# Unread transposes of the identity on the matmul engine while row norms are formed

## The chip, the cores and the metric

The kernel runs on one core of a Trainium2 chip. The metric is the device time of one execution in microseconds. TensorE (PE) multiplies matrices, VectorE (DVE) and ScalarE (ACT) do the elementwise work, GpSimd (POOL) here only forms powers, and SyncE (SP) issues the weight loads. [...]

## The reference

Two blocks of two layers each run over x of 256 rows by 1024 columns, all in float32. The joints of this case lie in the second block:

```
def second_block(x, ...):
    for l in range(DEPTH):                       # DEPTH = 2
        h = rms_norm_2(x, mix_pre_norm[l])
        m = hybrid_mixer(h, w_in[l], ...)        # 256x1024 -> 256x1024
        x = x + rms_norm_2(m, mix_post_norm[l])
        h = rms_norm_2(x, ffn_pre_norm[l])
        x = x + rms_norm_2(swiglu(h, ffn_gate[l], ffn_up[l], ffn_down[l]), ffn_post_norm[l])
    return x

def rms_norm_2(x, w):
    return x * rsqrt(mean(x * x, axis=-1) + 1e-6) * w
```

The mixer projects h to 13 groups of columns and more, runs a gated delta rule, a retention and a pooling branch, and multiplies their gated sum by w_out. Between the last product of one part and the first of the next lies a chain on which nothing else depends: row norm of the result, addition to x, row norm of x, transposition, scaling by the gain.

## The kernel before, in words

Each engine has its own program, and semaphores tie them together; nothing reorders an engine's list. x lies in SBUF as two tiles of 128 rows (t = 0 and 1). Weights come in units of four 128x512 pieces through a ring of slots that SP fills. Where precision asks for it, ACT rounds a unit (the `_hi` part, L954) and DVE subtracts it from the original (the `_rest` part, L1286), and PE then forms three products instead of one in `split_part` (L531 for groups whose result lies by column, L540 for the others). Each pair of the unit's pieces is a part, counted by the semaphore `w_split`.

PSUM has four banks `gp` for the large products and four banks `mp` for small steps. Small steps have names; `ORDER_1` and `ORDER_2` list them in the order in which PE runs them. The step with number n uses bank n % 4, and `begin` lets PE wait until the step n - 4 has been read (`step_read`). `end` raises `step_done` for the reader.

`x_transposes` carries out a joint on PE: the steps xT0, xT1 (tile t = 0, four 128x128 transposes each) when DVE has normed that tile (`x_normed`), xT2, xT3 for tile t = 1, and at its end it waits until all four banks are read. The steps fT0 to fT3 are the same before the feed-forward part. After it PE waits for `h_split`, then runs the matmuls of the next group (Q or F0, L531).

The other engines at a joint: DVE adds the result to x (`add_result`), ACT squares the rows (L961 and L1152), POOL forms the inverse root (L1916), and DVE scales the tile (L1402), reads each transposed step from PSUM with the gain (`normed_T`, L1280), and splits it into a rounded part and a rest (L1327, L1286), which raises `h_split`. In layer 0's first joint DVE reads xT0 and xT1 only after it has normed both tiles; at the other three it reads the first pair inside `add_result`, ahead of the norm of tile 1.

The last product before a joint runs t = 0 first and t = 1 second (`tail`, `split_tail`), so that tile 0 of x is ready while PE still works on tile 1.

Of the kernel before, what the change touches and what calls it, by code (L numbers as in the profile page):

```python
# [6 lines left out]
P = 128  # L7
# [4 lines left out]
DEPTH = 2  # L12
# [78 lines left out]
for _n, _name in enumerate(("do_g", "mq_g", "mk_g", "ho_g")):  # L91
# [6 lines left out]
    + ["om0", "om1", "hgo0", "hgo1"] + [f"sc{h}" for h in range(4)] + ["yT4", "yT5"] + [f"sc{h}" for h in range(4, 8)] + ["yT2", "yT3"] \  # L98
    + [f"pt{h}" for h in range(8)] + ["oa0", "oa1", "yT0", "yT1"]
BETWEEN = {1: ["rqT0", "rqT1", "rkT0", "rkT1"], 2: ["rs0", "rs1", "rs2"], 3: ["ro0", "ro1"], 4: ["pm0", "pm1"], 5: ["py0", "py1"]}  # L100
ORDER_2 = [f"xT{i}" for i in range(4)] + ["ba", "cg", "gb0", "gb1"] \
    + [f"bT{j}{t}" for j in range(3) for t in range(2)] \
    + ["kT0", "kT1", "qT0", "qT1", "kbT0", "kbT1", "mm0", "mm1", "at0", "at1"] \
    + ["mi0", "mi1"] \
# [1 line left out]
       for step in [f"{s}{n}_{t}" for s in ("Y", "Z", "W") for t in range(2) if not (s == "Z" and n == len(LEVELS) - 1)]  # L106
       + BETWEEN.get(n, [])] \
    + ["oT_r0", "oT_r1", "u0", "wT", "st", "vn1", "do0", "do1", "oT_d0", "oT_d1"] \
    + [f"yT{i}" for i in range(4)] + [f"fT{i}" for i in range(4)]
PRE = ["colA", "memT0", "memT1", "memT2", "memT3", "colB"]  # L110
STEPS = PRE + [f"A{l}.{s}" for l in range(DEPTH) for s in ORDER_1] + [f"B{l}.{s}" for l in range(DEPTH) for s in ORDER_2]
STEP_NO = {s: n for n, s in enumerate(STEPS)}
# [73 lines left out]
def mixer_program(nc, w, out):  # L186
# [6 lines left out]
    with ctx:  # L193
# [34 lines left out]
        ident, upper, ones = C("ident"), C("upper"), C("ones")  # L228
# [54 lines left out]
        xT3, cT3, e3 = region(b_x, 12, S), region(b_c, 12, S), region(b_e, 12, S)  # L283
# [11 lines left out]
        xs2 = region(b_e, TT, D)  # L295
# [42 lines left out]
        step_read = [sem(f"step_read{i}") for i in range(4)]  # L338
# [18 lines left out]
        def bank(step, *dims):  # L357
            v = mp[:, STEP_NO[step] % 4]
            if len(dims) == 2:
                n = dims[0] * dims[1]  # L360
                return v[:, 0:n].rearrange("p (a b) -> p a b", a=dims[0])
            return v[:, 0:dims[0]] if dims else v
# [114 lines left out]
        def _(pe):  # L477
            state = {"unit": 0, "step": 0}

            def begin(step, *waits):  # L480
                n = STEP_NO[step]
                assert n == state["step"], (step, STEPS[state["step"]])
                state["step"] += 1
                if n >= 4:
                    pe.wait_ge(step_read[n % 4], n // 4)
                for wait in waits:
                    pe.wait_ge(*wait)

            def end(ins):
                ins.then_inc(step_done, 1)  # L490
# [96 lines left out]
                    if t == 0:  # L587
                        last.then_inc(sig("first_tile"), 1)

            def x_transposes(names, src, n):  # L590
                for i in range(4):
                    t, q = divmod(i, 2)
                    transposes(names(i), [src[:, t, (4 * q + j) * P:(4 * q + j + 1) * P] for j in range(4)],
                               (sig("x_normed"), 2 * n + t + 1))
                for i in range(4):
                    pe.wait_ge(*read_out(names(i)))
# [13 lines left out]
            for l in range(DEPTH):  # L610
                s = lambda n: f"A{l}.{n}"
# [124 lines left out]
            for l in range(DEPTH):  # L736
                s = lambda n: f"B{l}.{n}"

                def group_in(g):
                    n = GROUP_NO[s(g)]  # L740
                    return group_read[n % 2], n // 2 + 1
                x_transposes(lambda i: s(f"xT{i}"), xs2, DEPTH + 2 * l)
                pe.wait_ge(sig("h_split"), 2 * TT * l + TT)
                for g in "QKV":
                    split_units(s(g), 2)
# [2 lines left out]
                for t in range(TT):  # L748
                    for k in range(KD):
                        for i, h_part in enumerate((mix_hT_hi, mix_hT_rest)):  # L750
                            last = nc.tensor.matmul(bank(s("ba"))[:, 16 * t:16 * t + 16], h_part[:, t, k, :], w_ba_parts[:, l, k, :],
                                                    start=(k == 0 and i == 0), stop=(k == KD - 1 and i == 1))
# [7 lines left out]
                for t in range(TT):  # L760
                    begin(s(f"gb{t}"), (sig("gates_ready"), l + 1))
                    for h in range(NH):
                        last = nc.tensor.matmul(bank(s(f"gb{t}"))[:, P * h:P * h + P], gbc[:, NH * t + h, :], upper, start=True, stop=True)
# [106 lines left out]
                last = len(LEVELS) - 1  # L870
# [35 lines left out]
                        pe.wait_ge(*read_out(s(f"yT{2 * j + t}")))  # L906
                sum_transposes(0)
                tail(4, lambda k, t: reg("B", f"G{2 + k // 4}")[:, t, P * (k % 4):P * (k % 4) + P], {2: lambda: sum_transposes(1)})
                x_transposes(lambda i: s(f"fT{i}"), xs2, DEPTH + 2 * l + 1)
                pe.wait_ge(sig("h_split"), 2 * TT * (l + 1))  # L910
                for j in range(FF_G):
                    split_units(s(f"F{j}"), 2)
# [1026 lines left out]
```

## Time and profile before

| | |
|---|---|
| median of 3 runs | 1636.79 us (1632.76 to 1643.85) |
| profiled execution, its own time | 1637.35 us |
| span of the profiled execution | 1635.5 us |
| PE busy | 1479.7 us, 90% |
| DVE busy | 966.3 us, 59% |
| ACT busy | 675.1 us, 41% |
| mean granted clock of PE | 0.958 |

PE's busy time includes matmuls that overlap, so their spacing in the timeline tells the pace and not the duration of one. An idle time in brackets stands before the instruction that ended it, with what released it.

The four joints are called A (before layer 0 of the second block, near 535 us), B (before layer 0's feed-forward part, near 880 us), C (before layer 1, near 1085 us) and D (before layer 1's feed-forward part, near 1430 us).

### The profile page before, as it was taken

Reading aid. Unit: us, or ns where it says so; the run is one execution under the profiler, and the core shown is the slowest. Engines: PE = TensorE matmul, PEld = TensorE weight load, DVE = VectorE, ACT = ScalarE, POOL = GpSimd, SP = SyncE. Lnnn points to the kernel's source line nnn. Section 1 sums busy time; section 2 is a strip of 40 time slices with the busy share of each in tenths; the row PEclk is TensorE's granted clock in tenths of the full one; section 3 lists DMA queues with packets and bytes.
Section 4 is the critical chain, followed back from the end, with each engine's and each line's share of the span. In section 5 each row is a group of like instructions: output and inputs, shape, how many; then the busy total and the mean of one; then the engine's idle time right before and its main releaser. Section 6 shows DMA issues by size and latency. Waiting matters only on the chain.

```text
span 1635.5 us, 20210 instructions
## 1 busy us (share of the span) xinstructions
PE 1479.7 (90%) x8410; PEld 1249.1 (76%) x8410; DVE 966.3 (59%) x1133; ACT 675.1 (41%) x901; POOL 50.2 (3%) x41
## 2 busy tenths in 40 slices
PE   5999987979889797999997999969889999889997
PEld 4977776868768786788654999869668866389986
DVE  7588664579664566755525566453885534265644
ACT  4565554465563455432213333325644221233332
POOL 0002000000100000000000000000000000000000
PEclk9999998989999898999998999989999999989999
DMA  7444223434333543333343655535333334435653
GB/s 247 156 130 152 78 83 123 157 127 134 100 102 116 174 154 104 103 104 108 124 154 111 186 186 188 181 119 171 129 103 104 122 109 163 146 109 186 186 176 115
DMA packets 138986, 225.80 MB, mean 138 GB/s; under 512 B 7889, under 2 KB 54289, under 8 KB 138769
## 3 DMA queue, kind: packets, MB, share of 16 engines
q1 hardware_dynamic: 133456, 221.60, 41.3%
q10 hardware_dynamic: 5440, 2.93, 0.6%
q8 instruction: 67, 1.10, 0.3%
q14 instruction: 23, 0.18, 0.0%
HBM read 223.46 MB, written 1.05 MB: 137 GB/s over the span
## 4 chain that ended last, share of the span: by engine, by line
PE 76%; DVE 13%; ACT 6%; issue 4%; POOL 1%; ACTq 0%; DMA 0%; POOLq 0%; DVEq 0%
PE gp L540 33%; PE gp L531 23%; PE gp L513 5%; PE mp L784 5%; PE gp L583 3%; DVE wt_rest L1286 3%; PE mp L630 2%; PE mp L495 2%; DVE arena L1722 2%; DVE arena L1280 2%; DVE hT L1280 1%; ACT arena L1028 1%; ACT arena L1168 1%; POOL rs_out L1916 1%; PE mp L684 1%
## 5 line engine op out<-in xcount | busy, mean ns | idle before, releaser
L531 PE MATMUL gp<-hT_hi,wt_hi 128*128 128x256 f32 x704 | 200.8, 285 | 6.9 <-DVE hT_rest L1286 6.9
L531 PE MATMUL gp<-hT_rest,wt_hi 128*128 128x256 f32 x704 | 200.4, 285 | 0.0
L531 PE MATMUL gp<-hT_hi,wt_rest 128*128 128x256 f32 x704 | 200.3, 284 | 0.0
L1286 DVE TENSOR_TENSOR wt_rest<-wt,mix_hi 128x1024 fp32r<-128x1024 f32 x120 | 141.5, 1221 | 96.5 <-ACT mix_hi L954 95.8
L1286 DVE TENSOR_TENSOR wt_rest<-wt,wt_hi 128x1024 fp32r<-128x1024 f32 x132 | 155.5, 1221 | 69.1 <-ACT wt_hi L954 69.1
L954 ACT ACTIVATE wt_hi<-wt 128x1024 fp32r<-128x1024 f32 x132 | 132.1, 1051 | 117.5 <-DMA wt<-in_ffn_up 58.8
L1286 DVE TENSOR_TENSOR wt_rest<-wt,first_hi 128x1024 fp32r<-128x1024 f32 x120 | 142.8, 1221 | 59.1 <-ACT first_hi L954 58.3
L954 ACT ACTIVATE first_hi<-wt 128x1024 fp32r<-128x1024 f32 x120 | 123.9, 1059 | 111.7 <-PE gp L540 98.1
L540 PE MATMUL gp<-mix_hi,mix_hT_hi 128*128 128x512 f32 x384 | 157.0, 409 | 4.3 <-DVE wt_rest L1286 4.3
L540 PE MATMUL gp<-wt_rest,mix_hT_hi 128*128 128x512 f32 x384 | 155.4, 405 | 0.0
L954 ACT ACTIVATE mix_hi<-wt 128x1024 fp32r<-128x1024 f32 x120 | 122.3, 1059 | 77.8 <-PE gp L540 48.0
L540 PE MATMUL gp<-mix_hi,mix_hT_rest 128*128 128x512 f32 x384 | 151.9, 396 | 0.0
L531 PEld LDWEIGHTS gp<-hT_hi,wt_hi 128*128 128x128 f32 x704 | 136.4, 194 | 7.7 <-issue 7.7
L495 PE MATMUL mp<-const,arena 128*128 128x128 f32 x512 | 81.4, 313 | 66.1 <-DVE arena L1402 25.4
L531 PEld LDWEIGHTS gp<-hT_rest,wt_hi 128*128 128x128 f32 x704 | 136.5, 194 | 0.0
L531 PEld LDWEIGHTS gp<-hT_hi,wt_rest 128*128 128x128 f32 x704 | 136.4, 194 | 0.0
L495 PEld LDWEIGHTS mp<-const,arena 128*128 128x128 f32 x512 | 69.2, 162 | 81.0 <-issue 45.9
L1280 DVE TENSOR_TENSOR arena<-arena,gp 128x512 f32<-128x512 f32 (+1 forms) x56 | 44.9, 802 | 136.3 <-ACT arena L1260 80.0
L934 ACT ACTIVATE arena<-gp 128x1024 f32<-128x1024 f32 x48 | 49.1, 1023 | 166.0 <-PE gp L540 166.0
L540 PE MATMUL gp<-first_hi,first_hT_hi 128*128 128x512 f32 x256 | 105.4, 412 | 4.2 <-DVE wt_rest L1286 4.2
L540 PE MATMUL gp<-wt_rest,first_hT_hi 128*128 128x512 f32 x256 | 103.6, 405 | 0.0
L540 PE MATMUL gp<-first_hi,first_hT_rest 128*128 128x512 f32 x256 | 102.5, 400 | 0.0
(270 smaller groups left out, 2890.5 us busy)
## 6 DMA issues: line engine op xcount, KB each, us to landing
wt<-in_w_in SPq DMA_DIRECT2D x100, 1024.0 KB, 5.1
wt<-in_ffn_gate SPq DMA_DIRECT2D x44, 512.0 KB, 3.9
wt<-in_ffn_up SPq DMA_DIRECT2D x44, 512.0 KB, 4.9
wt<-in_w_out SPq DMA_DIRECT2D x20, 1024.0 KB, 5.1
wt<-in_ffn_down SPq DMA_DIRECT2D x20, 1024.0 KB, 5.0
wt<-in_w_mem_kv SPq DMA_DIRECT2D x8, 1024.0 KB, 5.1
wt<-in_w_branch_pool SPq DMA_DIRECT2D x4, 1024.0 KB, 5.0
wt<-in_w_branch_ret SPq DMA_DIRECT2D x4, 1024.0 KB, 5.0
```

Source lines behind the costliest of these rows:

```text
L495: last = nc.tensor.transpose(bank(step)[:, P * j:P * j + P], tile, ident)
L513: last = nc.tensor.matmul(group_bank(group, t), stationary(k0 + k, t), wt[:, u % SLOTS, k, :], start=(k0 + k == 0), stop=(k0 + k == GROUPS ...
L531: last = nc.tensor.matmul(o, a[:, k, P * c:P * c + P], b[:, :, k0 + k, :], start=(k0 + k == 0 and c % 2 == 0 and i == 0), stop=(k0 + k == ...
L540: last = nc.tensor.matmul(group_bank(group, t), a, b[:, k, :], start=(kk == k_first and i == 0), stop=(kk == k_last and i == 2))
L583: last = nc.tensor.matmul(group_bank(GROUPS[g][0], t), stationary(k0 + k, t), wt[:, u % SLOTS, k, :], start=(k0 + k == 0), stop=(k0 + k == ...
L630: last = nc.tensor.matmul(bank(s(f"hg{n}_{t}"))[:, P * h:P * h + P], src_k[:, h, kt * P:kt * P + P], src_q[:, h, t * P:t * P + P], start=T ...
L784: last = nc.tensor.matmul(bank(step)[:, P * h:P * h + P], lhs(h), rhs(h), start=True, stop=True)
L934: nc.scalar.activation(dst, group_banks(name), func).then_inc(group_read[GROUP_NO[name] % 2], 1)
L954: nc.scalar.activation(rounded_part(u)[:, k:k + nk, :], wt[:, u % SLOTS, k:k + nk, :], ACT.Copy)\
L1280: return nc.vector.tensor_tensor(o, i0, i1, ALU.mult)
L1286: return nc.vector.tensor_tensor(o, i0, i1, ALU.subtract)
L1722: ins = nc.vector.scalar_tensor_tensor(cT3[:, k, d:], xT3[:, k, 0:S - d], taps[:, 3 - d, k:k + 1], cT3[:, k, d:], ALU.mult, ALU.add)
```

## The change

A new helper `keep_busy` transposes the identity into a bank of its own a given number of times. It is called between the second and third transposing step of each joint in the second block, and again behind the fourth. Two steps are added to the order at each joint, which shifts the bank numbers of the steps behind them. Nothing reads what `keep_busy` writes; its last pass itself raises `step_read`.

```
--- before.py
+++ after.py
@@ -98,7 +98,7 @@
     + ["om0", "om1", "hgo0", "hgo1"] + [f"sc{h}" for h in range(4)] + ["yT4", "yT5"] + [f"sc{h}" for h in range(4, 8)] + ["yT2", "yT3"] \
     + [f"pt{h}" for h in range(8)] + ["oa0", "oa1", "yT0", "yT1"]
 BETWEEN = {1: ["rqT0", "rqT1", "rkT0", "rkT1"], 2: ["rs0", "rs1", "rs2"], 3: ["ro0", "ro1"], 4: ["pm0", "pm1"], 5: ["py0", "py1"]}
-ORDER_2 = [f"xT{i}" for i in range(4)] + ["ba", "cg", "gb0", "gb1"] \
+ORDER_2 = ["xT0", "xT1", "xw0", "xT2", "xT3", "xw1"] + ["ba", "cg", "gb0", "gb1"] \
     + [f"bT{j}{t}" for j in range(3) for t in range(2)] \
     + ["kT0", "kT1", "qT0", "qT1", "kbT0", "kbT1", "mm0", "mm1", "at0", "at1"] \
     + ["mi0", "mi1"] \
@@ -106,7 +106,7 @@
        for step in [f"{s}{n}_{t}" for s in ("Y", "Z", "W") for t in range(2) if not (s == "Z" and n == len(LEVELS) - 1)]
        + BETWEEN.get(n, [])] \
     + ["oT_r0", "oT_r1", "u0", "wT", "st", "vn1", "do0", "do1", "oT_d0", "oT_d1"] \
-    + [f"yT{i}" for i in range(4)] + [f"fT{i}" for i in range(4)]
+    + [f"yT{i}" for i in range(4)] + ["fT0", "fT1", "fw0", "fT2", "fT3", "fw1"]
 PRE = ["colA", "memT0", "memT1", "memT2", "memT3", "colB"]
 STEPS = PRE + [f"A{l}.{s}" for l in range(DEPTH) for s in ORDER_1] + [f"B{l}.{s}" for l in range(DEPTH) for s in ORDER_2]
 STEP_NO = {s: n for n, s in enumerate(STEPS)}
@@ -587,8 +587,19 @@
                     if t == 0:
                         last.then_inc(sig("first_tile"), 1)
 
-            def x_transposes(names, src, n):
+            def keep_busy(step, passes):
+
+                begin(step)
+                for j in range(passes):
+                    last = nc.tensor.transpose(bank(step)[:, P * (j % 4):P * (j % 4) + P], ident, ident)
+                    if j == passes - 2:
+                        end(last)
+                last.then_inc(step_read[STEP_NO[step] % 4], 1)
+
+            def x_transposes(names, src, n, between=None):
                 for i in range(4):
+                    if i == 2 and between is not None:
+                        between()
                     t, q = divmod(i, 2)
                     transposes(names(i), [src[:, t, (4 * q + j) * P:(4 * q + j + 1) * P] for j in range(4)],
                                (sig("x_normed"), 2 * n + t + 1))
@@ -739,7 +750,8 @@
                 def group_in(g):
                     n = GROUP_NO[s(g)]
                     return group_read[n % 2], n // 2 + 1
-                x_transposes(lambda i: s(f"xT{i}"), xs2, DEPTH + 2 * l)
+                x_transposes(lambda i: s(f"xT{i}"), xs2, DEPTH + 2 * l, lambda: keep_busy(s("xw0"), 40 if l else 14))
+                keep_busy(s("xw1"), 28)
                 pe.wait_ge(sig("h_split"), 2 * TT * l + TT)
                 for g in "QKV":
                     split_units(s(g), 2)
@@ -906,7 +918,8 @@
                         pe.wait_ge(*read_out(s(f"yT{2 * j + t}")))
                 sum_transposes(0)
                 tail(4, lambda k, t: reg("B", f"G{2 + k // 4}")[:, t, P * (k % 4):P * (k % 4) + P], {2: lambda: sum_transposes(1)})
-                x_transposes(lambda i: s(f"fT{i}"), xs2, DEPTH + 2 * l + 1)
+                x_transposes(lambda i: s(f"fT{i}"), xs2, DEPTH + 2 * l + 1, lambda: keep_busy(s("fw0"), 40))
+                keep_busy(s("fw1"), 16)
                 pe.wait_ge(sig("h_split"), 2 * TT * (l + 1))
                 for j in range(FF_G):
                     split_units(s(f"F{j}"), 2)

```

PE's list at joint C before, from the first transposing step to the next group (`step_read` with a digit is the semaphore of that bank):

```order
L495 MATMUL mp<-const,arena 128x128 [waits x_normed,step_read3]
L495 MATMUL mp<-const,arena 128x128 x3
L495 MATMUL mp<-const,arena 128x128 [waits x_normed,step_read0]
L495 MATMUL mp<-const,arena 128x128 x3
L495 MATMUL mp<-const,arena 128x128 [waits x_normed,step_read1]
L495 MATMUL mp<-const,arena 128x128 x3
L495 MATMUL mp<-const,arena 128x128 [waits x_normed,step_read2]
L495 MATMUL mp<-const,arena 128x128 x3
L531 MATMUL gp<-mix_hT_hi,mix_hi_54 128x256 [waits h_split,step_read2,group_read0,step_read1,w_split,step_read0,step_read3]
```

And with the change:

```order
L495 MATMUL mp<-const,arena 128x128 [waits x_normed,step_read3]
L495 MATMUL mp<-const,arena 128x128 x3
L495 MATMUL mp<-const,arena 128x128 [waits x_normed,step_read0]
L495 MATMUL mp<-const,arena 128x128 x3
L594 MATMUL mp<-const 128x128 [waits step_read1]
L594 MATMUL mp<-const 128x128 x39
L495 MATMUL mp<-const,arena 128x128 [waits x_normed,step_read2]
L495 MATMUL mp<-const,arena 128x128 x3
L495 MATMUL mp<-const,arena 128x128 [waits x_normed,step_read3]
L495 MATMUL mp<-const,arena 128x128 x3
L594 MATMUL mp<-const 128x128 [waits step_read3,step_read2,step_read0]
L594 MATMUL mp<-const 128x128 x27
L531 MATMUL gp<-mix_hT_hi,mix_hi_54 128x256 [waits w_split,group_read0,h_split]
```

Forty passes stand before the second pair and 28 behind it; the waits for the reads of the first three or four banks (`step_read3`, `step_read2`, `step_read0`), which stood before the group's first matmul, now stand before the 28 passes, and the fourth transposing step waits for `step_read3`, the bank of the first.

At joint A, with the change:

```order
L495 MATMUL mp<-const,arena 128x128 [waits x_normed,step_read0]
L495 MATMUL mp<-const,arena 128x128 x3
L495 MATMUL mp<-const,arena 128x128 [waits x_normed,step_read1]
L495 MATMUL mp<-const,arena 128x128 x3
L594 MATMUL mp<-const 128x128 [waits step_read2]
L594 MATMUL mp<-const 128x128 x13
L495 MATMUL mp<-const,arena 128x128 [waits x_normed,step_read3]
L495 MATMUL mp<-const,arena 128x128 x3
L495 MATMUL mp<-const,arena 128x128 [waits x_normed,step_read0]
L495 MATMUL mp<-const,arena 128x128 x3
L594 MATMUL mp<-const 128x128 [waits step_read0,step_read3,step_read1]
L594 MATMUL mp<-const 128x128 x27
L531 MATMUL gp<-mix_hT_hi,mix_hi_54 128x256 [waits w_split,group_read0,h_split]
```

Here the first filler has 14 passes. The fourth transposing step waits for `step_read0`, the bank of this joint's first step.

## Rows read from the trace of the kernel before

**Rows 1.** The page: busy time, and the chain that ended last by engine.

```profile
PE 1479.7 (90%) x8410; PEld 1249.1 (76%) x8410; DVE 966.3 (59%) x1133; ACT 675.1 (41%) x901; POOL 50.2 (3%) x41
...
PE 76%; DVE 13%; ACT 6%; issue 4%; POOL 1%; ACTq 0%; DMA 0%; POOLq 0%; DVEq 0%
```

**Rows 2.** Timeline, PE at A to D: start us, us, engine, line, operation, count [idle before <-releaser].

```profile
535.62 1.94 PE L495 MATMUL mp<-const,arena 128*128 128x128 f32 x8 [3.38 <-DVE arena L1402]
...
543.38 0.55 PE L531 MATMUL gp<-mix_hT_hi,mix_hi 128*128 128x256 f32 x1 [5.82 <-DVE wt_rest L1286]
...
875.90 1.04 PE L495 MATMUL mp<-const,arena 128*128 128x128 f32 x8
...
884.26 1.94 PE L495 MATMUL mp<-const,arena 128*128 128x128 f32 x8 [7.33 <-DVE arena L1402]
...
889.68 0.55 PE L531 MATMUL gp<-hT_hi,wt_hi 128*128 128x256 f32 x1 [3.48 <-DVE hT_rest L1286]
...
1086.09 1.94 PE L495 MATMUL mp<-const,arena 128*128 128x128 f32 x8 [7.39 <-DVE arena L1402]
...
1093.75 0.55 PE L531 MATMUL gp<-mix_hT_hi,mix_hi 128*128 128x256 f32 x1 [5.72 <-DVE mix_hT_rest L1286]
...
1433.78 1.94 PE L495 MATMUL mp<-const,arena 128*128 128x128 f32 x8 [7.33 <-DVE arena L1402]
...
1439.17 0.55 PE L531 MATMUL gp<-hT_hi,wt_hi 128*128 128x256 f32 x1 [3.45 <-DVE hT_rest L1286]
```

**Rows 3.** Windows around joints A to D: stretch, busy us of each engine, PEclk, DMA.

```profile
535.00:547.00 12.00, 5.56 (x25) 5.22 (x26) 11.43 (x13) 2.65 (x3) 0.00 (x0) 0.50 0.36 132
...
880.00:892.00 12.00, 4.26 (x19) 3.92 (x20) 11.14 (x14) 6.83 (x8) 0.54 (x1) 0.50 0.06 20
...
893.00:895.00 2.00, 2.00 (x19) 2.00 (x18) 2.00 (x3) 0.00 (x0) 0.00 (x0) 1.00 0.03 8
...
1084.00:1097.00 13.00, 5.19 (x23) 4.85 (x24) 10.83 (x13) 2.10 (x4) 0.54 (x1) 0.50 0.07 21
...
1429.00:1442.00 13.00, 4.77 (x21) 4.43 (x22) 12.10 (x15) 6.83 (x8) 0.54 (x1) 0.50 0.10 34
```

**Rows 4.** Timeline, PE, matmuls of L531 in joint A.

```profile
543.73 0.41 PE L531 MATMUL gp<-mix_hT_rest,mix_hi 128*128 128x256 f32 x1
...
547.57 0.41 PE L531 MATMUL gp<-mix_hT_rest,mix_hi 128*128 128x256 f32 x1
...
548.33 0.28 PE L531 MATMUL gp<-mix_hT_hi,mix_hi 128*128 128x256 f32 x1
...
551.25 0.28 PE L531 MATMUL gp<-mix_hT_rest,mix_hi 128*128 128x256 f32 x1
```

**Rows 5.** Timeline, VectorE (DVE): last reads of transposed tiles in A, B, C.

```profile
538.70 1.41 DVE L1280 TENSOR_TENSOR hT<-mp,cols 128x512 f32<-128x512 f32 x2
...
885.89 1.41 DVE L1280 TENSOR_TENSOR hT<-mp,cols 128x512 f32<-128x512 f32 x2
...
1089.99 1.41 DVE L1280 TENSOR_TENSOR hT<-mp,cols 128x512 f32<-128x512 f32 x2
```

**Rows 6.** One line, L495: count, duration of one in ns, minimum/median/maximum.

```profile
L495 PE MATMUL mp<-const,arena x512: 270/273/477, 6.9 to 1435.3; 128*128 128x128 f32 x171
```

**Rows 7.** Timeline, PE, transposes elsewhere in the mixer of layer 0.

```profile
628.13 2.82 PE L495 MATMUL mp<-const,arena 128*128 128x128 f32 x12 [2.47 <-ACT arena L1200]
...
647.50 4.18 PE L495 MATMUL mp<-const,arena 128*128 128x128 f32 x24 [4.24 <-DVE arena L1280]
...
658.25 1.07 PE L495 MATMUL mp<-const,arena 128*128 128x128 f32 x8 [2.37 <-DVE arena L1280]
```

**Rows 8.** Windows over the stretches of rows 7.

```profile
628.00:633.00 5.00, 4.87 (x18) 4.39 (x19) 0.00 (x0) 4.63 (x8) 0.00 (x0) 0.50 0.00 0
...
647.00:650.00 3.00, 2.50 (x12) 2.53 (x13) 3.00 (x4) 1.12 (x2) 0.00 (x0) 0.50 0.23 89
...
651.00:652.00 1.00, 0.68 (x7) 0.45 (x5) 0.48 (x1) 1.00 (x3) 0.00 (x0) 1.00 0.06 16
```

More of the change, by code:

```diff
@@ L100 @@
 BETWEEN = {1: ["rqT0", "rqT1", "rkT0", "rkT1"], 2: ["rs0", "rs1", "rs2"], 3: ["ro0", "ro1"], 4: ["pm0", "pm1"], 5: ["py0", "py1"]}
-ORDER_2 = [f"xT{i}" for i in range(4)] + ["ba", "cg", "gb0", "gb1"] \
+ORDER_2 = ["xT0", "xT1", "xw0", "xT2", "xT3", "xw1"] + ["ba", "cg", "gb0", "gb1"] \
     + [f"bT{j}{t}" for j in range(3) for t in range(2)] \
@@ L108 @@
     + ["oT_r0", "oT_r1", "u0", "wT", "st", "vn1", "do0", "do1", "oT_d0", "oT_d1"] \
-    + [f"yT{i}" for i in range(4)] + [f"fT{i}" for i in range(4)]
+    + [f"yT{i}" for i in range(4)] + ["fT0", "fT1", "fw0", "fT2", "fT3", "fw1"]
 PRE = ["colA", "memT0", "memT1", "memT2", "memT3", "colB"]
@@ L588, in tail, with keep_busy, x_transposes @@
                         last.then_inc(sig("first_tile"), 1)
-            def x_transposes(names, src, n):
+            def keep_busy(step, passes):
+                begin(step)
+                for j in range(passes):
+                    last = nc.tensor.transpose(bank(step)[:, P * (j % 4):P * (j % 4) + P], ident, ident)
+                    if j == passes - 2:
+                        end(last)
+                last.then_inc(step_read[STEP_NO[step] % 4], 1)
+            def x_transposes(names, src, n, between=None):
                 for i in range(4):
+                    if i == 2 and between is not None:
+                        between()
                     t, q = divmod(i, 2)
@@ L741, in group_in @@
                     return group_read[n % 2], n // 2 + 1
-                x_transposes(lambda i: s(f"xT{i}"), xs2, DEPTH + 2 * l)
+                x_transposes(lambda i: s(f"xT{i}"), xs2, DEPTH + 2 * l, lambda: keep_busy(s("xw0"), 40 if l else 14))
+                keep_busy(s("xw1"), 28)
                 pe.wait_ge(sig("h_split"), 2 * TT * l + TT)
@@ L908, in _ @@
                 tail(4, lambda k, t: reg("B", f"G{2 + k // 4}")[:, t, P * (k % 4):P * (k % 4) + P], {2: lambda: sum_transposes(1)})
-                x_transposes(lambda i: s(f"fT{i}"), xs2, DEPTH + 2 * l + 1)
+                x_transposes(lambda i: s(f"fT{i}"), xs2, DEPTH + 2 * l + 1, lambda: keep_busy(s("fw0"), 40))
+                keep_busy(s("fw1"), 16)
                 pe.wait_ge(sig("h_split"), 2 * TT * (l + 1))
```

## The prediction

> **What bounds the kernel now.** I read the page first: the matmul engine (PE) is busy for 90% of the span, and the chain that ended last runs on PE for 76% of it [rows 1]. So PE's own pace and its idle time at the joints set the end. Then I read PE in order of time around the four joints that the change touches. I call them A (into layer 0 of the second block), B (into layer 0's feed-forward part), C (into layer 1) and D (layer 1's feed-forward part). Each has the same shape: eight transposes right behind the last matmul, idle, eight transposes, idle, then the dense matmuls of L531 [rows 2]. The first idle stretch is 3.38 us in A and 7.33 to 7.39 us in the others. The second is 5.82, 3.48, 5.72 and 3.45 us.
>
> [...] What half a clock costs shows in the spacing of the L531 matmuls: 18 steps from 543.73 to 547.57 us are 0.213 us each, 25 steps from 548.33 to 551.25 us are 0.117 us each [rows 4]. So each matmul issued at half clock loses 0.096 us. In A the half-clock matmuls last from 543.38 to about 547.9 us, which is 21 of them; in C, where the stretch at 0.50 reaches past 1097 us, from 1093.75 to about 1097.4 us, 17; in B from 889.68 to about 892.7 us, 14; in D I take 14 too, since it starts like B. That is 66 such matmuls, **6.4 us, the most that a held clock could give back**. The slow second group of transposes (1.94 us for eight against 1.04 us [rows 2]) costs nothing: VectorE reads it only later, at 538.70, 885.89 and 1089.99 us [rows 5].
>
> **What is added.** 222 transposes: 14 + 28 in A, 40 + 16 in B, 40 + 28 in C, 40 + 16 in D. Eight existing ones take 1.04 us and one alone 0.27 us, so the seven steps between them are 0.110 us each at the full clock; at half clock eight take 1.94 us and one 0.48 us, 0.209 us a step, and I take the 0.213 us of the matmuls [rows 2, 4, 6]. Nothing reads the results, so a pass costs only what it delays on PE.
>
> *First filler (14 or 40 passes).* At full clock, where it starts because PE was dense until then, it takes 1.5 us in A (room 3.38) and 4.4 us in B, C and D (room 7.3). It delays nothing. At half clock throughout, 40 passes would be 8.5 us, 1.2 us more than the room, and half of that would reach VectorE, which takes the tile 1.6 us after its release in B [rows 2, 5]; behind dense work I take the full clock and cost it at nothing. The extra step also moves the PSUM bank of the steps behind it: the last of the four real transposes now waits until the first one's bank is read. VectorE reads that bank while the second pair is being prepared, or sooner, so this is nothing as well.
>
> *Second filler (28 or 16 passes).* It stands behind the waits for all four reads, so it can't start when PE goes idle, only when VectorE has read the last bank: 538.70 + 1.41 = 540.1 us in A, 887.3 us in B, 1091.4 us in C [rows 5]. From there to the first matmul of before there are 3.2, 2.4 and 2.35 us; D is as B. At 0.110 us, 28 passes are 3.1 us and 16 are 1.8 us: covered in A, B and D, but **0.75 us too long in C**. At half clock 28 passes are 6.0 us and 16 are 3.4 us, and all four joints are late, by 2.7, 1.0, 3.6 and 1.0 us. Behind the filler on PE stand the matmuls, and behind these the whole chain; no other engine waits for the filler.
>
> **Does the clock stay up?** With the filler at full clock PE's idle times become: A 1.9, then 3.5 us before the second filler; B and D 2.9, then 2.0; C 3.0, then 4.3. The trace has comparable gaps. 2.37 us of idle behind dense work left the clock up: the eight transposes after it take 1.07 us. 2.47 us elsewhere did not, nor did 3.38 and 4.24 us [rows 2, 7, 8]. So in A and C I expect the clock to fall in the second gap, which the change leaves open, and in B and D it is a toss-up. Once down, transposes alone do bring it back: 24 of them start at 647.50 us at 0.50, and it is at 1.00 by 651 us [rows 7, 8]. From the start of work to the return it is about 3 us there, about 3, 4 and 4.5 us in B, C and A, and over 5 us at 628 us; I take 3.7 us.
>
> [...]
>
> **The sum, joint by joint.**
> - A, clock down: 17 passes in 3.7 us, 11 more at 0.110 us, so the filler ends at 545.05. The 21 matmuls then run at full clock to 547.5; before, they ended at 543.38 + 21 x 0.213 = 547.85. **-0.35 us**.
> - C, clock down: the filler ends at 1096.3, 17 matmuls end at 1098.3 against 1097.4 before. **+0.9 us**.
> - B: with the clock held, 14 x 0.096 = -1.35 us. With it down, 16 half-clock passes end at 890.7, one half-clock matmul and 13 at full clock end at 892.45 against 892.65: -0.2 us. Half and half: **-0.8 us**. D the same, **-0.8 us**.
>
> Together -1.05 us. Nothing downstream takes it back or adds to it, as PE runs on without a wait after each joint for tens of microseconds. Made against the profiled execution, 1637.35 us becomes 1636.3 us; that execution stands 0.56 us above the median of 1636.79 us, so the median would be 1635.7, **about 1636 us: no change that can be measured**. A measurement of this kernel tells about 1% from no change, 16 us, and all cases lie inside it.
>
> **The rivals.**
> 1. *The clock is held at all four joints.* For it: 2.37 us of idle was bridged, and both fillers shorten the gaps. Against: 3.5 and 4.3 us stay open in A and C. It gives -2.0 in A, -1.35 in B and in D, and -1.65 + 0.75 = -0.9 in C: -5.6 us, **1631 us**.
> 2. *Slower: transposes of the identity neither hold nor restore the clock, so the second filler runs at half clock and is itself the delay.* The matmuls behind it start slow as before. It decides as soon as a pass takes over 0.115 us in A, 0.147 us in B and D (cover by number of passes); C is past its point already. Price 2.7 + 1.0 + 3.6 + 1.0 = +8.3 us, **1645 us**. [...] Against it: the 24 transposes at 647.50 us; for it, only that those read data and these read one constant tile.
> 3. *The passes are slow at any clock*, because weights and moving data come from the same 128 columns of SBUF, which no row shows. The same +8.3 us, but dense filler holds or restores the clock, -6.4 us: about +2 us, **1639 us**.
>
> **Numbers.** Chances: the sum 0.60, rival 1 0.20, rival 2 0.12, rival 3 0.08. The runs differ among themselves: half-clock stretches elsewhere in the kernel fall anew in each execution, and the three runs of before span 1632.76 to 1643.85 us; so each case has some 3 us on either side. The range of 1629 to 1643 us takes in the first, most of the second and the last, and leaves out the larger part of rival 2. Faster by over 1% (below 1620 us) would take more than twice what the slow matmuls cost in all: 0.02. Slower by over 1% (above 1653 us) takes rival 2 and more: 0.03. Within 1%: 0.95.
>
> **What would show it.** 222 transposes that read only the constants; the first filler of 14 or 40 at 0.110 us a pass; the second starting right behind VectorE's last read of a transposed tile; in A and C a clock of 0.50 when it starts and of 1.00 when L531 starts, with L531 1.7 and 2.6 us later behind that read than before; in B and D either a clock of 1.00 throughout or a fall in the second gap. Spacing of the first L531 matmuls at 0.117 us shows that the clock came back. I am wrong if the spacing of the filler is not 0.110 us at full clock, if a new wait of VectorE on PE appears at the bank that is used again, or if the gain or loss lies outside these four joints.

## The result, and the profile after

| | before | changed |
|---|---|---|
| median of 20 runs each | 1637.47 us | 1643.67 us |
| lowest to highest | 1632.76 to 1643.85 | 1639.22 to 1649.91 |
| ratio, 95% interval | | 1.0036, 1.0023 to 1.0049 |
| span of the profiled execution | 1635.5 us | 1644.4 us |

The change costs about 6 us (3.8 to 8.0 us by the interval). That is less than the 1% named in the prediction, but its sign is clear of the noise, and the median lies 0.7 us above the range that was given. Two executions far above all the others, one of the kernel before at 1830.8 us and one of a variant below at 5264 us, are in no ratio.

The page of the changed kernel, its busy line, answers to [rows 1]: 222 more matmuls and as many more weight loads, 30 us more of busy time for each, and no other engine moved by more than 1 us.

```profile
PE 1509.3 (92%) x8632; PEld 1278.6 (78%) x8632; DVE 966.4 (59%) x1133; ACT 675.5 (41%) x901; POOL 49.2 (3%) x41
```

The timeline of PE in joints A, B and C of the changed kernel answers to [rows 2] (the columns are the same; D is as B; L594 is the filler):

```profile
533.50 1.69 PE L594 MATMUL mp<-const 128*128 128x128 f32 x14
537.05 1.16 PE L495 MATMUL mp<-const,arena 128*128 128x128 f32 x8 [1.86 <-DVE arena L1415]
541.79 5.29 PE L594 MATMUL mp<-const 128*128 128x128 f32 x28 [3.58 <-DVE hT L1293]
...
881.27 4.53 PE L594 MATMUL mp<-const 128*128 128x128 f32 x40
888.77 1.06 PE L495 MATMUL mp<-const,arena 128*128 128x128 f32 x8 [2.96 <-DVE arena L1415]
892.07 3.65 PE L594 MATMUL mp<-const 128*128 128x128 f32 x16 [2.24 <-DVE hT L1293]
...
1083.86 4.53 PE L594 MATMUL mp<-const 128*128 128x128 f32 x40
1091.62 1.48 PE L495 MATMUL mp<-const,arena 128*128 128x128 f32 x8 [3.22 <-DVE arena L1415]
1097.18 5.77 PE L594 MATMUL mp<-const 128*128 128x128 f32 x28 [4.09 <-DVE hT L1293]
```

The first fillers run at full clock: 40 passes take 4.53 us, 0.11 us each. The second pair of transposes in B then runs at full clock too (1.06 us, not 1.94). But PE idles again until VectorE's last read, and the second filler takes 3.65 us for 16 passes, 0.213 us each. The windows over these stretches, with the same columns as [rows 3], say why (PEclk, the last figure but two, is the granted clock as a share of full speed): in B the clock is at 1.00 beside the first filler and the transposes and at 0.50 beside the second filler, and it is at 0.50 beside the second filler of A and C too.

```profile
541.00:546.00 5.00, 4.21 (x20) 4.24 (x21) 4.93 (x6) 0.00 (x0) 0.00 (x0) 0.50 0.00 0
547.00:549.00 2.00, 2.00 (x19) 2.00 (x18) 1.06 (x1) 0.00 (x0) 0.00 (x0) 1.00 0.00 0
881.00:886.00 5.00, 4.80 (x44) 4.56 (x42) 3.35 (x6) 1.13 (x5) 0.54 (x1) 1.00 0.79 261
889.00:890.00 1.00, 0.83 (x8) 0.59 (x6) 0.96 (x2) 1.00 (x2) 0.00 (x0) 1.00 0.00 0
891.00:897.00 6.00, 4.93 (x23) 4.96 (x24) 5.90 (x7) 1.56 (x2) 0.00 (x0) 0.50 0.00 1
898.00:900.00 2.00, 2.00 (x19) 2.00 (x18) 2.00 (x3) 0.00 (x0) 0.00 (x0) 1.00 0.00 0
1092.00:1102.00 10.00, 5.91 (x30) 5.54 (x29) 9.05 (x10) 0.00 (x0) 0.00 (x0) 0.51 0.00 0
```

So in B the filler pushes the first L531 matmul to 895.37 us, 15.0 us behind the joint's first transpose (13.8 before), and the matmuls still begin at half clock, ten of them:

```profile
895.37 0.56 PE L531 MATMUL gp<-hT_hi,wt_hi 128*128 128x256 f32 x1
895.73 0.41 PE L531 MATMUL gp<-hT_rest,wt_hi 128*128 128x256 f32 x1
...
897.85 0.28 PE L531 MATMUL gp<-hT_hi,wt_hi 128*128 128x256 f32 x1
897.97 0.28 PE L531 MATMUL gp<-hT_rest,wt_hi 128*128 128x256 f32 x1
```

To follow the 6 us I cut the span into parts, from starts on PE's timeline. A *joint* is the time from its first transpose to the 60th matmul behind its first L531 matmul; behind the joints lie *mixer 0* (A to B), *mixer 1* (C to D) and the two feed-forward stretches. These, from B to C and from D to the start of PE's last matmul, were 179.39 and 179.16 us within 0.01 us in every profile and are left out. The table has all eight profiles of the two kernels and those of the variants below, in us.

| profile | A | B | C | D | joints | mixer 0 | mixer 1 |
|---|---|---|---|---|---|---|---|
| before | 21.34 | 22.37 | 24.87 | 22.37 | 90.95 | 323.36 | 322.88 |
| before, 2nd | 21.08 | 23.56 | 25.57 | 22.44 | 92.65 | 326.84 | 323.57 |
| before, 3rd | 20.99 | 22.37 | 24.88 | 22.39 | 90.63 | 322.88 | 322.84 |
| before, 4th | 21.35 | 22.37 | 25.13 | 23.54 | 92.39 | 323.37 | 326.78 |
| changed | 21.48 | 23.20 | 26.82 | 23.15 | 94.65 | 326.29 | 323.65 |
| changed, 2nd | 21.45 | 23.16 | 26.96 | 23.09 | 94.66 | 326.36 | 323.59 |
| changed, 3rd | 21.45 | 23.16 | 26.96 | 23.08 | 94.65 | 326.32 | 323.64 |
| changed, 4th | 21.47 | 23.24 | 26.90 | 23.32 | 94.93 | 326.26 | 326.62 |
| steps only | 21.09 | 23.40 | 25.50 | 22.34 | 92.33 | 326.88 | 323.68 |
| first filler only | 21.02 | 22.21 | 24.88 | 22.25 | 90.36 | 322.92 | 322.98 |
| second filler only | 21.30 | 23.04 | 26.83 | 23.08 | 94.25 | 323.39 | 323.62 |
| second filler short | 19.82 | 22.39 | 24.94 | 22.36 | 89.51 | 324.75 | 322.90 |
| second filler early | 19.28 | 22.52 | 24.85 | 22.34 | 88.99 | 323.96 | 323.45 |
| second filler doubled | 24.13 | 24.94 | 28.97 | 24.99 | 103.03 | 326.46 | 326.36 |
| dense | 19.28 | 21.03 | 23.39 | 21.05 | 84.75 | 326.17 | 325.71 |
| dense, 2nd | 19.28 | 21.03 | 23.57 | 21.06 | 84.94 | 323.96 | 322.81 |
| dense, mixers too | 19.46 | 21.03 | 23.18 | 21.04 | 84.71 | 323.02 | 322.39 |

By the means of four profiles each, the change adds 0.27, 0.52, 1.80 and 0.47 us in A to D, 3.1 us together, and 2.2 and 0.4 us in the two mixers. The stretch ahead of joint A, which the change doesn't touch, was 530.4 us before and 531.5 after, with 529.4 to 532.6 among the eight; four profiles a side can't tell this 1.1 us from chance.

### The profile page after: what moved, and what is told of

It reads as the page before. It is cut to its first block, busy times and chain, and to the rows that moved or that the text cites. A ratio compares the mean times of both kernels' runs of the same rounds, so it can differ in the third digit from the quotient of the medians.

```text
span 1644.4 us, 20654 instructions
## 1 busy us (share of the span) xinstructions
PE 1509.3 (92%) x8632; PEld 1278.6 (78%) x8632; DVE 966.4 (59%) x1133; ACT 675.5 (41%) x901; POOL 49.2 (3%) x41
## 3 DMA queue, kind: packets, MB, share of 16 engines
HBM read 223.46 MB, written 1.05 MB: 137 GB/s over the span
## 4 chain that ended last, share of the span: by engine, by line
PE 77%; DVE 12%; ACT 5%; issue 3%; POOL 1%; ACTq 0%; DMA 0%; POOLq 0%; DVEq 0%
PE gp L540 33%; PE gp L531 22%; PE gp L513 5%; PE mp L796 4%; PE gp L583 3%; DVE wt_rest L1299 3%; PE mp L495 2%; PE mp L641 2%; DVE arena L1735 2%; DVE arena L1293 2%; PE mp L594 1%; DVE hT L1293 1%; ACT arena L1041 1%; POOL rs_out L1929 1%; PE mp L695 1%
## 5 line engine op out<-in xcount | busy, mean ns | idle before, releaser
L531 PE MATMUL gp<-hT_hi,wt_hi 128*128 128x256 f32 x704 | 200.4, 285 | 0.0
L531 PE MATMUL gp<-hT_rest,wt_hi 128*128 128x256 f32 x704 | 200.0, 284 | 0.0
L531 PE MATMUL gp<-hT_hi,wt_rest 128*128 128x256 f32 x704 | 200.0, 284 | 0.0
L540 PE MATMUL gp<-mix_hi,mix_hT_hi 128*128 128x512 f32 x384 | 157.7, 411 | 4.4 <-DVE wt_rest L1299 4.4
L540 PE MATMUL gp<-wt_rest,mix_hT_hi 128*128 128x512 f32 x384 | 155.9, 406 | 0.0
L540 PE MATMUL gp<-mix_hi,mix_hT_rest 128*128 128x512 f32 x384 | 152.2, 396 | 0.0
L531 PEld LDWEIGHTS gp<-hT_hi,wt_hi 128*128 128x128 f32 x704 | 136.2, 194 | 0.0
L531 PEld LDWEIGHTS gp<-hT_rest,wt_hi 128*128 128x128 f32 x704 | 136.0, 193 | 0.0
L531 PEld LDWEIGHTS gp<-hT_hi,wt_rest 128*128 128x128 f32 x704 | 136.0, 193 | 0.0
L495 PE MATMUL mp<-const,arena 128*128 128x128 f32 x512 | 79.7, 309 | 51.4 <-DVE arena L1293 13.2
L495 PEld LDWEIGHTS mp<-const,arena 128*128 128x128 f32 x512 | 67.9, 159 | 66.3 <-issue 31.4
L540 PE MATMUL gp<-first_hi,first_hT_hi 128*128 128x512 f32 x256 | 105.5, 412 | 4.2 <-DVE wt_rest L1299 4.2
L540 PE MATMUL gp<-wt_rest,first_hT_hi 128*128 128x512 f32 x256 | 103.5, 404 | 0.0
L540 PE MATMUL gp<-first_hi,first_hT_rest 128*128 128x512 f32 x256 | 102.5, 400 | 0.0
```

The source lines that it names most:

```text
L495: last = nc.tensor.transpose(bank(step)[:, P * j:P * j + P], tile, ident)
L531: last = nc.tensor.matmul(o, a[:, k, P * c:P * c + P], b[:, :, k0 + k, :], start=(k0 + k == 0 and c % 2 == 0 and i == 0), stop=(k0 + k == ...
L540: last = nc.tensor.matmul(group_bank(group, t), a, b[:, k, :], start=(kk == k_first and i == 0), stop=(kk == k_last and i == 2))
```

## The experiments

Theory 1: the second filler, which can start only when VectorE has read the last bank, meets a clock that has just fallen, runs at half clock for longer than the time that hides it, and delays all behind it. The rivals were the added steps and waits themselves, and work on PE that slows the chain beside it. All edits are against the changed kernel, and each ratio is against the kernel before as it ran beside the variant: 12 executions of each variant (5 of the doubled one, 7 of the last one), 12 to 35 of the kernel before.

**Steps only.** Fillers of 2 passes.

```
-  lambda: keep_busy(s("xw0"), 40 if l else 14)); keep_busy(s("xw1"), 28)
+  lambda: keep_busy(s("xw0"), 2));               keep_busy(s("xw1"), 2)
   ... fw0, fw1 likewise 2
```

> Both fillers of every joint cut to 2 passes (16 instead of 222 in all), so that the two added steps, the moved bank numbers and the moved waits stay, and the work goes. Theory 1 (the second filler, which starts only behind VectorE's last read and then runs at half clock, is what is late): within 2 us of the kernel before, each joint from its first transpose to the 60th L531 matmul within 0.3 us of before (21.3, 22.4, 24.9, 22.4 us). Rival 2 (the steps and waits themselves cost, through the banks of the mixer): +5 to +6 us as with the change. Rival 3 (PE work in the first gap slows the chain beside it): as before, since there is none.

Measured: ratio 1.0007 (0.9993 to 1.0022). The added steps, their waits and the moved banks cost nothing that can be seen. The joints of this one profile came out 1.4 us above the first profile of before and not within 0.3 us each; the second and fourth profiles of the kernel before show the same 92.4 to 92.7 us.

**First filler only.**

```
-  keep_busy(s("xw1"), 28)   keep_busy(s("fw1"), 16)
+  keep_busy(s("xw1"), 2)    keep_busy(s("fw1"), 2)
```

> The first filler of each joint as in the change (14 or 40 passes), the second cut to 2. Theory 1: within 2 us of before; the clock still falls in the second gap of each joint, and the first L531 matmuls run at half clock as before. Rival 2: +5 to +6 us. Rival 3 (the first filler slows ScalarE, VectorE or the weight loads beside it): +3 us or more, with a longer stretch from the first to the third transposing step than 11.5 us less 3.1 us in B.

Measured: 1.0000 (0.9986 to 1.0014), joints 90.36 us. The first filler is free, and useless: the clock falls behind it, in the second gap (in B 10.0 us behind the joint's first transpose, with the gap from 9.4 to 11.7 us). Its 134 passes beside the norms delay nothing: in B the second pair of transposes starts 8.4 us behind the first, as before.

**Second filler only.**

```
-  keep_busy(s("xw0"), 40 if l else 14)   keep_busy(s("fw0"), 40)
+  keep_busy(s("xw0"), 2)                 keep_busy(s("fw0"), 2)
```

> The second filler as in the change (28 or 16 passes), the first cut to 2. Theory 1: nearly all of the change's cost, +4 to +6 us; the joints from first transpose to the 60th L531 matmul 0.1, 0.8, 1.9 and 0.8 us longer than before in A to D, because the passes run at 0.213 us. Rival 2: +5 to +6 us too, but then the first variant shows it as well. Rival 3: within 2 us of before.

Measured: 1.0029 (1.0014 to 1.0043), 4.7 us, with joints of 94.25 us. The cost of the change in the joints is here, and joint by joint it is that of the change within 0.2 us. In this variant the clock falls in the first gap already. In B it has been down for 5.1 us when the filler starts at 887.01 us, and it is at half for 5.1 us more:

```profile
887.01 3.65 PE L594 MATMUL mp<-const 128*128 128x128 f32 x16 [1.36 <-DVE hT L1293]
```

```profile
882.00:892.00 10.00, 6.93 (x32) 6.59 (x33) 9.20 (x11) 5.50 (x6) 0.54 (x1) 0.50 0.01 2
893.00:895.00 2.00, 2.00 (x19) 2.00 (x18) 2.00 (x3) 0.00 (x0) 0.00 (x0) 1.00 0.00 0
```

**Second filler doubled.**

```
-  keep_busy(s("xw1"), 28)   keep_busy(s("fw1"), 16)
+  keep_busy(s("xw1"), 56)   keep_busy(s("fw1"), 32)
```

> The change with its second filler doubled (56 and 32 passes). Theory 1: the passes stand in PE's list with nothing beside them, so all that is added is paid: 28 more passes at the full clock, to which it has come back by then, are +3.1 us in A and in C, and 16 more are about +1.9 us in B and D; +10 us on the change, +16 us on the kernel before, ratio about 1.010. Were the cost in the added steps or in the first filler, doubling the second would change nothing: ratio 1.003 to 1.004.

Measured: 1.0089 (1.0070 to 1.0108), 14.6 us. The joints are 8.4 us above those of the change. In B and D the 16 added passes are paid in full at 0.11 us, +1.8 us each. In A and C the 28 added passes cost 2.7 and 2.1 us and not 3.1, because in this profile the clock returned earlier, at 12.5 and 17.4 us behind the joint's first transpose instead of 13.3 and 19.3.

**Second filler short.**

```
-  keep_busy(s("xw1"), 28)                  keep_busy(s("fw1"), 16)
+  keep_busy(s("xw1"), 10 if l else 14)     keep_busy(s("fw1"), 10)
```

> The first filler as in the change, the second cut to what fits behind VectorE's last read at half clock: 14 passes (3.0 us) in A and 10 (2.1 us) in B, C and D. Theory 1: L531 starts as early as before in every joint, and the clock returns 1 to 2 us earlier for it, so 1 to 4 us faster than before (1633 to 1636 us). Rival 2: +4 to +6 us. Rival 3: +3 us.

Measured: 0.9992 (0.9979 to 1.0006); joints 89.51 us. No delay is left. The gain I had expected with it, an earlier return of the clock, appears in A alone (19.82 us); in B, C and D the joints are as before.

**Second filler early**, with the same numbers of passes, ahead of the waits for the reads.

```
 def x_transposes(names, src, n, between=None, behind=None):
     ...
+    if behind is not None:
+        behind()                  # the second filler
     for i in range(4):
         pe.wait_ge(*read_out(names(i)))
```

> The change with its own numbers of passes (14 and 28, 40 and 16, 40 and 28, 40 and 16), only the second filler moved ahead of the four waits for VectorE's reads. Theory 1: the second filler then runs at full clock right behind the transposes and ends 2.6 to 3.6 us before the matmuls are released, so it delays nothing; the clock still falls behind it in most joints or shortly before L531. No cost, and none or little gain: ratio 0.998 to 1.0005. If instead the number of passes itself were what costs, wherever they stand: +3 to +6 us as with the change.

Measured: 0.9991 (0.9979 to 1.0002). The very 222 passes of the change cost nothing once the second filler stands ahead of the waits: in B its 16 passes take 1.91 us, and 2.58 us of idle are left ahead of the release of L531. A gains (19.28 us); in B, C and D the clock falls within 1 us of the start of L531 (0.3 and 0.8 us behind it in B and C, 0.4 us ahead of it in D), and the joints are as before.

```profile
881.68 1.07 PE L495 MATMUL mp<-const,arena 128*128 128x128 f32 x8 [2.96 <-DVE arena L1417]
882.58 1.91 PE L594 MATMUL mp<-const 128*128 128x128 f32 x16
887.08 0.36 PE L531 MATMUL gp<-hT_hi,wt_hi 128*128 128x256 f32 x1 [2.58 <-DVE hT_rest L1301]
```

**Dense.** The same place, with as many passes as the gaps hold at full clock.

```
-  lambda: keep_busy(s("xw0"), 40 if l else 14)), keep_busy(s("xw1"), 28)
+  lambda: keep_busy(s("xw0"), 60 if l else 26), lambda: keep_busy(s("xw1"), 54))
-  lambda: keep_busy(s("fw0"), 40)),              keep_busy(s("fw1"), 16)
+  lambda: keep_busy(s("fw0"), 60),              lambda: keep_busy(s("fw1"), 36))
```

> The second filler is moved ahead of the four waits for VectorE's reads, so that it starts right behind the fourth transposing step, and both fillers are sized to fill their gaps at full clock: 26 and 54 passes in A, 60 and 36 in B, 60 and 54 in C, 60 and 36 in D. Theory 1 (gaps of 2 us and more let the clock fall, and only that makes a pass dear): the clock stays at 1.00 through all four joints, L531 starts when it did before and at 0.117 us a matmul, so each joint from its first transpose to the 60th L531 matmul is 1.3 to 2 us shorter than before (about 19.4, 21.0, 23.1 and 21.0 us) and the whole 5 to 7 us faster, ratio 0.996 to 0.997. Rival 2 of the prediction (transposes of the identity don't hold the clock): the clock falls in the joints although PE never idles for 2 us, the passes take 0.213 us and the kernel is 15 us or more slower. Rival 3 (PE work beside the norms slows VectorE or ScalarE): the first L531 matmul comes 1 us or more later behind the first transpose than in the kernel before.

The windows over the four joints of this variant: the clock is at 1.00 throughout.

```profile
530.00:545.00 15.00, 13.97 (x114) 12.79 (x113) 11.53 (x18) 4.94 (x6) 0.55 (x1) 1.00 0.63 227
875.00:891.00 16.00, 14.82 (x119) 13.07 (x117) 11.62 (x17) 8.11 (x12) 1.08 (x2) 1.00 0.42 135
1075.00:1095.00 20.00, 18.43 (x153) 17.48 (x152) 14.89 (x20) 6.20 (x10) 1.50 (x3) 1.00 0.51 179
1424.00:1441.00 17.00, 15.79 (x123) 13.71 (x122) 12.56 (x18) 8.10 (x12) 1.08 (x2) 1.00 0.44 138
```

And B on PE's timeline, 60 and 36 passes at 0.11 us, with L531 released by VectorE 13.8 us behind the first transpose, as before:

```profile
877.23 1.04 PE L495 MATMUL mp<-const,arena 128*128 128x128 f32 x8
878.11 6.71 PE L594 MATMUL mp<-const 128*128 128x128 f32 x60
885.60 1.06 PE L495 MATMUL mp<-const,arena 128*128 128x128 f32 x8 [0.78 <-DVE arena L1417]
886.50 4.09 PE L594 MATMUL mp<-const 128*128 128x128 f32 x36
891.00 0.36 PE L531 MATMUL gp<-hT_hi,wt_hi 128*128 128x256 f32 x1 [0.40 <-DVE hT_rest L1301]
```

The joints are 84.75 us, 6.9 us under the mean of before, as expected; rival 2 of the prediction falls, and so does rival 3 of the expectation, since L531 is not late. The 2 us of the expectation were an estimate, and no run shows a limit there: the gaps left in these joints, 0.40 to 0.87 us, kept the clock, 2.24 us behind an idle time of 2.96 us in B and D of the change did not, and single gaps of 2.37 and 2.36 us in the two mixers of the first profile of before did. The whole was only 0.9985 (0.9971 to 0.9998), 2.5 us faster. In its profile the joints gained 6.2 us on the first profile of before and the mixers lost 5.6 us; whether the second comes of the first was the next question.

**The mixers.** Second profiles, with the code unchanged, asked whether their length belongs to a kernel or to an execution.

> The kernel before, once more, for the spread of its parts: the two feed-forward stretches between joints within 0.05 us of 179.4 and 179.2 us; the joints (first transpose to the 60th L531 matmul) within 0.5 us of 21.3, 22.4, 24.9 and 22.4 us; the mixers' stretches anywhere between 322 and 327 us, if what differs there is only when the clock falls.

> The dense variant once more. The joints again 19.3, 21.0, 23.4 and 21.0 us, with the clock at 1.00 in all. If the mixers of this variant were 2.8 us longer in its first profile only because of where the clock fell, they come out elsewhere between 322 and 327 us; if the held clock in a joint brings on the falls in the mixer, both are above 325 us again.

> The change once more. Theory 1: joints A to D again near 21.5, 23.2, 26.8 and 23.2 us, 3 to 4 us more than before together; the mixers anywhere between 322 and 327 us. If the change itself lengthens the mixers, by the moved PSUM banks: both again above 323.5 us, and together 3 us or more above the second look at the kernel before.

The dense variant came out with mixers of 646.8 us instead of 651.9 together, and the kernel before with 650.4 instead of 646.2: in these two the length belongs to the execution. So the gain of the dense variant is not taken back by rule; why its 12 runs show 2.5 us and not 6 or 7 stays open, beyond that the mixers scatter by more than that. The change gave 649.9 us again, so two more pairs followed.

> A third profile of the change. Joints together 94 to 95 us as in the first two (94.65 and 94.66). If the mixers are lengthened by the change, their two stretches are again 649.9 us together, as in both profiles so far; if it is only the place of the clock's falls, they come out elsewhere between 646 and 652 us in this or the next.

> A fourth profile of the change: joints together 94 to 95 us; mixers together 649.9 us if the change fixes them, elsewhere between 646 and 652 us if not.

> A third profile of the kernel before. Joints together 91 to 93 us as in the first two (90.95 and 92.65); each mixer's stretch one of the values seen, 322.9 to 326.9 us.

> A fourth profile of the kernel before: joints together 91 to 93 us, mixers together between 646 and 651 us.

Mixer 0 of the change stayed at 326.3 us four times out of four, where the kernel before had 322.9, 323.4, 323.4 and 326.8. Mixer 1 of the change was 323.6 three times and 326.6 once, like before. The moved banks alone don't make the mixers long: the variants with the first or the second filler alone have the same steps and banks as the change, and mixer 0 took 322.92 and 323.39 us in them. What the lengths stand for shows in windows over mixer 0. First the kernel before in its third profile, then the change in its first:

```profile
650.00:655.00 5.00, 3.23 (x29) 3.04 (x28) 4.80 (x7) 1.65 (x2) 0.00 (x0) 1.00 0.01 3
662.00:665.00 3.00, 3.00 (x15) 2.41 (x14) 2.50 (x3) 1.06 (x1) 0.00 (x0) 1.00 0.53 132
```

```profile
650.00:655.00 5.00, 5.00 (x24) 4.70 (x24) 3.29 (x4) 3.26 (x6) 0.00 (x0) 0.50 0.00 0
662.00:665.00 3.00, 3.00 (x10) 2.41 (x8) 2.90 (x5) 0.00 (x0) 0.00 (x0) 0.51 0.00 0
```

Behind an idle time of 4.4 us the same 24 transposes run wholly at half clock in the change (5.35 us) and only in part in the kernel before (4.25 us), and a later gap brings a second fall:

```profile
649.34 5.35 PE L495 MATMUL mp<-const,arena 128*128 128x128 f32 x24 [4.42 <-DVE arena L1293]
654.62 4.10 PE L790 MATMUL mp<-arena 128*128 128x128 f32 x32
661.15 1.12 PE L495 MATMUL mp<-const,arena 128*128 128x128 f32 x8 [2.44 <-DVE arena L1293]
```

```profile
644.77 4.25 PE L495 MATMUL mp<-const,arena 128*128 128x128 f32 x24 [4.41 <-DVE arena L1280]
```

A fall at this place marks every long mixer. In all 34 mixers of the table's 17 profiles, the window from 108.6 to 109.6 us behind the mixer's start has the clock at 0.50 where the mixer took 325.7 us or more, and at 1.00 where it took 324.8 us or less.

**Dense, mixers too.** If the mixers' gaps are what scatters them, fillers there should gather them.

```
-  + ["kT0", "kT1", ...            + ["mi0", "mi1"]
+  + ["kw", "kT0", "kT1", ...      + ["mw", "mi0", "mi1"]
   ...
   split_units(s("PU"), 2)
+  keep_busy(s("kw"), 34)
   ...
+  keep_busy(s("mw"), 16)          # ahead of the mi transposes
```

> The dense variant, and in the mixer of each layer two more fillers: 34 passes ahead of the transposes of k (PE idles 4.2 us there in the kernel before) and 16 ahead of the first transposes of the inversion (2.4 us). Theory 1: the joints as in the dense variant, and in the mixers the stretch at half clock behind the longer gap goes, where 24 transposes took 4.2 instead of 2.8 us; 1 to 3 us for two layers, so 3 to 6 us faster than before, ratio 0.996 to 0.998. If the clock's falls in the mixer only move elsewhere (to the many matmuls of 16 columns or to a gap left open): as the dense variant, 0.9985.

Measured: **0.9949** (0.9931 to 0.9968), 1630.45 us against 1638.56: better than expected, 8.4 us faster than before and faster than every other variant. Its seven executions lie between 1626.98 and 1631.03 us, where the 12 of the kernel before beside it span 1633.57 to 1644.10 us, so the times are gathered too. The windows over both stretches are at 1.00:

```profile
638.00:654.00 16.00, 14.27 (x120) 13.37 (x120) 15.56 (x17) 5.96 (x9) 0.00 (x0) 1.00 0.20 67
1183.00:1199.00 16.00, 14.33 (x118) 13.29 (x117) 14.98 (x17) 5.95 (x9) 0.54 (x1) 1.00 0.26 84
```

The clock still falls elsewhere in the mixers: in mixer 0 it is at 0.50 from 585 to 588 us and from 622.5 to 629 us. The one profile is of the fastest of the seven executions, and 2.5 us of its gain on the mean of before lie ahead of joint A, where no filler stands.

## Why the prediction was wrong

- *What bounds it, and the price of half a clock* were right. In [rows 3] the clock is at 0.50 in all four joints and at 1.00 from 893 to 895 us in B, and the L531 matmuls of A stand 0.213 us apart up to 547.57 us, within its half clock, and 0.117 us apart from 548.33 us on, behind it [rows 4]. 6.4 us was named as the most that a held clock could return, from [rows 3, 4]; the dense variant's joints are 6.9 us under the mean of before and 6.2 under the profile that the sum was made against.
- *First filler and added steps at nothing*: right, ratios 1.0000 and 1.0007.
- *The second filler starts only behind the last read*: right, and it is the whole of the cost in the joints. Its room was taken a little too large from [rows 5]: it started 3.0 us ahead of the old start of L531 in A, 2.1 in B and D and 1.9 in C, not 3.2, 2.4 and 2.35, counted from the joint's first transpose.
- *The clock in A and C falls*: right. In A it fell in the second gap, 6.5 us behind the joint's first transpose; in C already beside the second pair of transposes, at 9.1 us, 0.5 us behind the first gap. *The toss-up in B and D* was the first step that failed. The clock fell in both, in all four profiles of the change and in the three variants with the same first filler and gap (first filler only, second short, second doubled). Taking the mean of the two cases had put 0.6 us of gain too much on each. The gap of 2.24 us there follows 2.96 us of idle and 1.06 us of transposes; the single gap of 2.37 us in [rows 7] was no measure for it.
- *"I take 3.7 us" from the start of work to the clock's return* was the second, and the larger one. It came out at 4.2 us in A, 5.5 in B, 5.2 in C and 5.4 in D. So ten L531 matmuls of B ran at half clock, where the sum had one, and the 28 passes of C took 5.8 us and not 4.9. Why the return took longer than in the rows that were averaged stays open. How long the clock had been down doesn't settle it: it had fallen 1.3 us ahead of the second filler in B and 5.1 us ahead in C, and with the second filler only 5.1 us ahead in B and 8.6 us in C, and the return took 5.1 to 5.5 us in all four. Measured from the joint's first transpose, in the first profile of each kernel, the clock returned at 16.8 us before and 17.2 after in B, 19.8 and 19.4 in C, 16.8 and 17.1 in D; only in A was it 16.7 and 13.4. (The kernel before varies too: 19.5 us in B and 21.4 in C in its second profile, whose joints there are the longest.) The fillers of B, C and D bought next to no earlier return, and delayed L531 by 1.2, 3.6 and 1.2 us (the sum had 1.0, 2.6 and 1.0); in A an earlier return and a delay of 2.0 us cancel. In place of -0.35, -0.8, +0.9 and -0.8 us for A to D the profiles show +0.3, +0.5, +1.8 and +0.5: 3.1 us instead of -1.05.
- *"Nothing downstream takes it back or adds to it"* failed for mixer 0. The reason given for it, that PE runs on without a wait behind each joint, holds as far as it goes. In the kernel before, from the first matmul of L531, PE has no idle time of 0.02 us or more for 65.7 us behind A and 65.3 us behind C, for 189.0 us behind B (up to joint C's first gap), and behind D for 187.8 us, up to the start of its last matmul. Then L540 waits 0.81 us for VectorE's `wt_rest` behind A, at 609.1 us, and 0.80 us behind C, at 1159.1 us. But further on in the mixers PE waits again, for 2.5, 4.2 and 2.4 us in mixer 0 [rows 7]. Where the clock falls there depends on the execution (in the four profiles of before it falls a second time 73.9, 76.7, 76.9 and 73.9 us behind the start of mixer 0), and the change puts it at one of the worse places every time seen: 2.2 us over the mean of before. That joint A, where the clock returns 0.9 us ahead of L531 in each profile of the change, sets this is an inference, and one profile speaks against it: the variant with the second filler alone has the same A, and its mixer 0 took 323.39 us. What sets it stays open; four profiles a side can't exclude that some of it is chance.
- *The rivals.* The third (passes slow at any clock) falls with 0.11 us a pass at a clock of 1.00. The second had the mechanism of the loss, half-clock passes behind the last read, but for a wrong reason: transposes of the identity did hold the clock and restore it here. The dense variant shows the first, with 85 us of joints, little but transposes in their gaps, at 1.00. Joint A of the change shows the second: the clock returned beside the second filler, 4.2 us behind its start and 0.9 us ahead of L531. The first rival would have needed gaps closed, which the change left open: 1.9 and 3.6 us in A, 3.0 and 2.2 us in B and D, 3.2 and 4.1 us in C.
- *The range* leaned on the scatter of single runs. The case with the second filler late in all four joints was there, as rival 2 at +8.3 us and 1645 us, but the range ended below it. That the measured 1643.67 us comes near 1645 is luck: the joints lost 3.1 us, and the rest lies in mixer 0 and outside the stretches that rival 2 counted.

## What to carry to other kernels

What held the clock here was filler ahead of the wait that it bridges, sized at the full-clock pace of 0.11 us a pass, that filled the gap but for 0.4 to 1.2 us: in the three profiles of the dense variants the four joints are at 1.00. Where it stopped 2.2 us or more short in B, C and D, the clock fell behind it: that cost nothing (ratios 1.0000, 0.9992 and 0.9991), but it gained nothing in these joints either. Filler behind the wait delayed the next work by every pass that its room didn't hold, and ran at whatever clock the gap had left: 0.213 us a pass at 0.50, 0.11 us at 1.00. Where an execution's half-clock stretches wander, as they did in these mixers (322.8 to 326.8 us in one kernel), time many runs, and compare profiles part by part; one profile each would have blamed or acquitted the wrong stretch here.

## What the runs showed of the hardware that was not expected

- The clock fell while PE was busy. In each mixer 32 matmuls of 16 columns follow one another at 0.11 us; PE counts as fully busy (3.00 of 3.00 us), and behind them or beside the last of them the clock falls to half in 31 of the 34 mixers of these profiles. It does not in mixer 0 of the second dense profile and of the early filler, nor in mixer 1 of the first dense one. In the kernel before, where it fell in all eight:

```profile
585.00:588.00 3.00, 3.00 (x29) 3.00 (x29) 0.25 (x1) 0.00 (x0) 0.00 (x0) 1.00 0.55 161
589.00:592.00 3.00, 3.00 (x9) 2.33 (x8) 0.40 (x3) 2.42 (x5) 0.00 (x0) 0.50 0.13 50
```

- In B and D, 2.96 and 2.24 us of idle (2.23 to 2.27 us in the second gap) with 1.06 us of transposes between them were followed by a fall of the clock in 14 of 14 cases. A single idle time of 2.37 us behind dense work, in the mixer of the kernel before, was not in its first profile, and one of 2.44 us in mixer 0 of the change was.
- A mixer of the same kernel before took 322.8 to 326.8 us from one profiled execution to the next, and the longest were those in which the clock fell once more behind the gap of 2.4 us (107.3 and 107.4 us behind the mixer's start in the two of 326.8 us).
